# Mixture-of-experts stage: the small products between the weight slots, in four groups an expert

## The reference

```python
def swiglu(h, w_gu, w_down):
    gt, up = jnp.split(h @ w_gu, 2, axis=-1)
    return (jax.nn.silu(gt) * up) @ w_down

def moe(h, w_r, b_r, w_gu, w_down):
    t = h.reshape(-1, shp[-1])
    logits = (t @ w_r).astype(jnp.float32) + b_r.astype(jnp.float32)
    top_v, top_i = lax.top_k(logits, TOP_K)          # TOP_K = 2
    wts = jax.nn.softmax(top_v, axis=-1)
    comb = jnp.sum(jax.nn.one_hot(top_i, N_EXPERTS) * wts[..., None], axis=1)
    out = jnp.zeros_like(t)
    for e in range(N_EXPERTS):                       # 8 experts
        out = out + comb[:, e:e + 1] * swiglu(t, w_gu[e], w_down[e])
    return out.reshape(shp)
```

## Time and profile before

| what | value |
|---|---|
| median of three executions | 1933.45 us |
| the profiled execution, its time | 1935.77 us |
| its span, first to last instruction | 1933.7 us |
| mean granted clock of TensorE | 0.985 |
| TensorE matmul busy (whole program) | 1884.3 us, 97% |
| VectorE, ScalarE, GpSimd busy | 745.0, 453.5, 240.8 us |
| the eight experts | 946.15 to 1908.94 us of the span |

### The profile page before, as it was taken

The page is one execution under the profiler, slowest core; times in us unless marked ns, Lnnn a source line. Parts: engine busy times, 40 slices in busy tenths (PEclk is TensorE's granted clock), DMA queues, the critical chain, the costliest instruction groups (busy, mean ns, idle before and its releaser), DMA issues.

```text
span 1933.7 us, 55829 instructions
## 1 busy us (share of the span) xinstructions
PE 1884.3 (97%) x25022; PEld 1383.8 (72%) x25022; DVE 745.0 (39%) x1602; ACT 453.5 (23%) x852; POOL 240.8 (12%) x281
## 2 busy tenths in 40 slices
PE   7999999999999999999999999999999999999997
PEld 3777998999998778998655566555665556655564
DVE  5896448655584896357500101001010010100112
ACT  2214335445432215343300100101001000010011
POOL 2540423000003450432100000000000000000000
PEclk9999998999999999999999999999999999999998
DMA  9576445555552465445599999999999999999992
GB/s 357 181 268 246 142 159 175 196 185 176 183 180 93 144 218 198 146 137 186 205 376 392 361 375 337 376 392 361 375 336 378 393 357 375 335 379 398 361 365 70
DMA packets 143141, 525.48 MB, mean 272 GB/s; under 512 B 16192, under 2 KB 16704, under 8 KB 142272
## 3 DMA queue, kind: packets, MB, share of 16 engines
q1 hardware_dynamic: 140544, 508.82, 71.8%
q10 hardware_dynamic: 1728, 7.85, 1.2%
q0 software_dynamic: 640, 5.35, 0.8%
HBM read 515.52 MB, written 6.43 MB: 270 GB/s over the span
## 4 chain that ended last, share of the span: by engine, by line
PE 92%; DVE 4%; DMA 1%; issue 1%; ACT 1%; SPq 0%; ACTq 0%; DVEq 0%
PE bank L1057 46%; PE bank L913 13%; PE bank L297 9%; PE bank L653 8%; PE bank L517 4%; PE bank L533 2%; PE bank L999 2%; PE bank L1067 1%; PE bank L482 1%; PE bank L1010 1%; DMA masks<-in_masks 1%; PE bank L897 1%; PE bank L459 0%; PE bank L727 0%; DMA ring<-in_w 0%
## 5 line engine op out<-in xcount | busy, mean ns | idle before, releaser
L1057 PE MATMUL bank<-ring,gx 128*32 128x256 f32 x10752 | 599.9, 380 | 0.0
L1057 PEld LDWEIGHTS bank<-ring,gx 128*32 128x32 f32 x10752 | 340.0, 110 | 228.5 <-issue 8.0
L1057 PE MATMUL bank<-ring,arena 128*32 128x256 f32 x5376 | 296.5, 379 | 0.0
L1057 PEld LDWEIGHTS bank<-ring,arena 128*32 128x32 f32 x5376 | 172.3, 110 | 114.2 <-issue 1.3
L2418 DVE TENSOR_TENSOR arena<-arena,bank 128x128 f32<-128x128 f32 x168 | 38.3, 283 | 487.6 <-ACT arena L1548 487.6
L297 PE MATMUL bank<-hT,ring 128*128 128x264 f32 x864 | 204.8, 397 | 4.5 <-issue 2.5
L297 PEld LDWEIGHTS bank<-hT,ring 128*128 128x128 f32 x864 | 166.3, 195 | 40.3 <-issue 11.4
L913 PE MATMUL bank<-hh,whi 128*128 128x264 f32 x448 | 128.6, 287 | 1.3 <-DVE hl L2449 1.0
L2329 DVE COPY arena<-bank 32x256 f32<-32x256 f32 x27 | 11.5, 427 | 301.6 <-PE bank L1057 301.3
L913 PE MATMUL bank<-hh,wlo 128*128 128x264 f32 x448 | 127.5, 285 | 0.0
L913 PE MATMUL bank<-hl,whi 128*128 128x264 f32 x448 | 127.4, 284 | 0.0
(11 more groups left out here) (425 smaller groups left out, 2684.8 us busy)
## 6 DMA issues: line engine op xcount, KB each, us to landing
ring<-in_w SPq DMA_DIRECT2D x964, 512.0 KB, 5.7
out_gdns<-arena POOLq DMA_DIRECT2D x2, 2048.0 KB, 8.3
arena<-in_gdn ACTq DMA_DIRECT2D x2, 1536.0 KB, 7.1
xT<-in_x ACTq DMA_DIRECT2D x1, 1056.0 KB, 9.2
out_y<-hT SPq DMA_DIRECT2D x4, 264.0 KB, 2.1
arena<-in_gdn ACTq DMA_DIRECT2D x2, 512.0 KB, 3.9
masks<-in_masks ACTq DMA_DIRECT2D x1, 512.0 KB, 11.3
cpk<-in_cpk SPq DMA_DIRECT2D x1, 512.0 KB, 6.6
```

The costliest lines, as they stand in the source:

```text
L1057: ins = pe.matmul(o[32 * j:32 * j + 32, 0:DQ], x(t), w[:, DQ * c:DQ * c + DQ], start=first, stop=last)
```

## The change

The small products are put together in four groups an expert (five in odd experts but the last): behind slot 4 the return of m = 0 to 4; behind slot 20 turns 0 and 1 and the return of m = 5 to 7; behind slot 36 turns 2 and 3 and DCT; behind down slot 4 (slot 60) turns 4 to 6 and, where another pair follows, gathers 0 and 1; behind down slot 8 (slot 64) gathers 2 and 3. The products of a group go to different banks (BACK_BANK, TURN_BANK, DCT_BANK, GATHER_BANK), some of them banks of the chunk that is not being written, so new waits stand ahead of chunks 1, 3 and 5 and of the down slots. `erow` gets a third buffer. Expert 0 returns nothing, and the last expert gathers nothing; the zeroed rows and weights ahead of expert 0 are gone. (The further passes keep both.)

```diff
-        TURN = 3
         ROWS = 0
-        COMBINE = range(4, 8)
-        DCT = 9
+        BACK = {4: (0, 1, 2, 3, 4), 20: (5, 6, 7)}
+        BACK_BANK = (6, 7, 3, 4, 5, 3, 4, 5)
+        TURN = {20: (0, 1), 36: (2, 3), UP_S + 4: (4, 5, 6)}
+        TURN_BANK = (6, 7, 6, 7, 6, 7, 0)
+        DCT, DCT_BANK = 36, 3
-        GATHER = range(UP_S + 6, UP_S + 14, 2)
+        GATHER = {UP_S + 4: (0, 1), UP_S + 8: (2, 3)}
+        GATHER_BANK = (1, 2, 6, 7)
...
             for e in range(NE):
-                body(e, e, e // 2, e, e % 2, None)
-            body.finish(NE)
+                body(e, e - 1, e // 2, e, e % 2, None)
+            body.finish(NE - 1)
...
@@ TensorE: gather, combine
-                    if i >= 2:
-                        pe.wait_ge(sem("gx_done"), pg * 4 + (i - 1))
...
-                    pe.wait_ge(sem("down_taken"), g * KD + (KD + m - 1))
...
@@ TensorE: expert
+                returns = a is not None or q > 0
+                ahead = a is None and sub and e < NE - 1
...
+                def between(s):
+                    if TURN.get(s, (0,))[0]:
+                        pe.wait_ge(sem("turned_done"), q * NCH + TURN[s][0])
+                    for c in TURN.get(s, ()):
+                        turn(c)
+                    if s in BACK and BACK[s][0] == 0 and sub == 0:
+                        pe.wait_ge(sem("gx_done"), pg * 4 + 4)
+                    for m in BACK.get(s, ()) if returns else ():
+                        self.combine(m, g, bank[BACK_BANK[m]])
+                    if s == DCT:
+                        pe.wait_ge(sem("dw_done"), g * 3 + 6)
+                        for t in range(3):
+                            m = P if t < 2 else NB
+                            ins = pe.transpose(bank[DCT_BANK][0:CAP, P * t:P * t + m], dw[0:m, t, :], ident[0:m, 0:m])
+                        ins.then_inc(sem("dcT_full"), 1)
+                    if ahead and s in GATHER:
+                        if GATHER[s][0]:
+                            pe.wait_ge(sem("turned_done"), q * NCH + 6)
+                        for i in GATHER[s]:
+                            self.gather(i, pg + 1)
...
-                    if c == 1 and k == 0:
+                    if c == 1 and k == 0 and returns:
                         pe.wait_ge(sem("e_ys"), g * 2 + 2)
+                        pe.wait_ge(sem("down_taken"), g * KD + (KD + 5))
...
+                    if c == 3 and k == 0 and returns:
+                        pe.wait_ge(sem("down_taken"), g * KD + 2 * KD)
+                    if c == 5 and k == 0:
+                        pe.wait_ge(sem("dcT_done"), q * 1 + 1)
                     slot_products(s, lambda t: gx[:, k, mine + 32 * t:mine + 32 * t + 32], k == 0, k == KD - 1)
-                    if k == TURN and c:
-                        turn(c - 1)
...
+                    between(s)
                 for f in range(FT):
...
                     if f == 0:
-                        pe.wait_ge(sem("dcT_done"), q * 1 + 1)
+                        pe.wait_ge(sem("act_done"), q * NCH + (FT + 1 + NCH - 1))
...
+                    between(s)
@@ ScalarE, VectorE: the same lists, one slot later
-                    for c in turned_after(m):
+                    for c in TURN.get(m - 1, ()):
...
-                    if m - 1 in COMBINE:
-                        for k in (2 * (m - 1 - COMBINE[0]), 2 * (m - 1 - COMBINE[0]) + 1):
-                            self.add(k, g)
+                    for k in BACK.get(m - 1, ()) if a is not None or q else ():
+                        self.add(k, g, bank[BACK_BANK[k]])
...
-                        if sub:
+                        if a is None and sub and e < NE - 1:
                             self.choose(e + 1, a)
```

More of the change, by code:

```diff
@@ L224, in trunk_program @@
         at_e = 2 * B1 + NCH * TT * P
-        erow = ar(at_e, 2, TT, P)
-        srow = ar(at_e + 2 * TT * P, 2, TT, P)
-        ys = ar(at_e + 4 * TT * P, D)
+        erow = ar(at_e, 3, TT, P)
+        srow = ar(at_e + 3 * TT * P, 2, TT, P)
+        ys = ar(at_e + 5 * TT * P, D)
         ring2 = over("ring2", [P, ERING - RING, SLOT * P], where(whi), 0, F32)
-        yh = over("yh", [P, D], arena_at, at_e + 5 * CH)
+        yh = over("yh", [P, D], arena_at, at_e + 6 * CH)
         yl = over("yl", [P, D], slab_at, QT * (3 + N) + KD * N + 4)
[L231 to L234, removed]
+        dcT = over("dcT", [P, N], arena_at, at_e + 6 * CH + D)
+        dsel = over("dsel", [P, 3, PAIR], arena_at, at_e + 6 * CH + D + N)
+        dw = ar(at_e + 6 * CH + D + N + 3 * PAIR, 3, CAP)
+        iota = ar(at_e + 6 * CH + D + N + 3 * PAIR + 3 * CAP, PASSES * CAP)
         def col(l, name, i=0, w=None):
@@ L1002, in gather, with combine @@
                     ins.then_inc(sem("gather_full"), 1)
-                def combine(self, m, g):
+                def combine(self, m, g, b):
                     if m == 0:
                         pe.wait_ge(sem("ye_done"), g * 2 + 2)
-                    pe.wait_ge(sem("down_taken"), g * KD + (KD + m - 1))
-                    pe.matmul(bank[6 + m % 2][:, 0:N], yh[:, m * P:(m + 1) * P], dcT[:, :], start=True, stop=False)
-                    pe.matmul(bank[6 + m % 2][:, 0:N], yl[:, m * P:(m + 1) * P], dcT[:, :],
+                    pe.matmul(b[:, 0:N], yh[:, m * P:(m + 1) * P], dcT[:, :], start=True, stop=False)
+                    pe.matmul(b[:, 0:N], yl[:, m * P:(m + 1) * P], dcT[:, :],
                               start=False, stop=True).then_inc(sem("down_full"), 1)
                 def begin(self, g, pg, a):
-                    for i in range(4):
-                        self.gather(i, pg)
+                    if a is None:
+                        for i in range(4):
+                            self.gather(i, pg)
                 def end(self, g, a):
                     for m in range(KD):
-                        self.combine(m, g)
+                        pe.wait_ge(sem("down_taken"), g * KD + (KD + m - 1))
+                        self.combine(m, g, bank[6 + m % 2])
                     pe.wait_ge(sem("down_taken"), g * KD + 2 * KD)
@@ L1063, in turn @@
                     pe.wait_ge(sem("act_done"), q * NCH + (FT + 1 + c + 1))
-                    if c:
-                        pe.wait_ge(sem("turned_done"), q * NCH + c)
                     for r in range(TT):
-                        ins = pe.transpose(bank[6][:, P * r:P * r + P], erow[:, c % 2, r, :], ident)
+                        ins = pe.transpose(bank[TURN_BANK[c]][:, P * r:P * r + P], erow[:, c % 3, r, :], ident)
                     ins.then_inc(sem("turned_full"), 1)
+                def between(s):
[18 more added lines that the diff above has]
+                            self.gather(i, pg + 1)
+                if a is not None and sub == 0:
+                    for i in range(4):
+                        self.gather(i, pg)
                 mine = CAP * sub
@@ L1074, in expert @@
                     if sub == 0 and c == 0 and k % 2 == 0:
-                        pe.wait_ge(sem("gx_done"), pg * 4 + (k // 2 + 1))
-                    if c == 1 and k == 0:
+                        pe.wait_ge(sem("gx_done"), pg * 4 + max(k // 2 + 1, 2))
+                    if c == 1 and k == 0 and returns:
                         pe.wait_ge(sem("e_ys"), g * 2 + 2)
+                        pe.wait_ge(sem("down_taken"), g * KD + (KD + 5))
                     if c >= 2 and k == 0:
                         pe.wait_ge(sem("act_done"), q * NCH + (FT + 1 + c - 1))
+                    if c == 3 and k == 0 and returns:
+                        pe.wait_ge(sem("down_taken"), g * KD + 2 * KD)
+                    if c == 5 and k == 0:
+                        pe.wait_ge(sem("dcT_done"), q * 1 + 1)
                     slot_products(s, lambda t: gx[:, k, mine + 32 * t:mine + 32 * t + 32], k == 0, k == KD - 1)
-                    if k == TURN and c:
-                        turn(c - 1)
[L1083 to L1094, removed]
+                    between(s)
                 for f in range(FT):
@@ L1524, in begin @@
                 def begin(self, g, pg, a):
-                    for i in range(4):
-                        self.gathered(i, pg)
+                    if a is None:
+                        for i in range(4):
+                            self.gathered(i, pg)
                 def end(self, g, a):
@@ L1541, in expert @@
                 for m in range(FFN_S + 1):
-                    if m == ROWS:
+                    if m == 0 and a is not None and sub == 0:
+                        for i in range(4):
+                            self.gathered(i, pg)
+                    if m == ROWS and (a is not None or q):
                         self.rows(g, q, a)
@@ L2325, in rows @@
                     v.wait_ge(sem("ywt_done"), g + 1)
[L2326 to L2327 removed]
+                    v.wait_ge(sem("e_used"), q * FFN_S)
                     for r in range(TT):
@@ L2338, in low, with add @@
```

(17 more changed lines are left out.)

42 lines of the change are left out of this document (17 added, 25 removed).

## The result

The changed kernel takes 1901.95 us (median); before it are 1932.6 us (1931.24 to 1934.53). The ratio is 0.9838 with a 95% interval of 0.9824 to 0.9852, so the change is worth about 31 us. 1904.5 was forecast, within 1900 to 1914. The ratio leaves out one of the four executions of the changed kernel, which ran at a lower clock and took 2082.3 us; the median counts it.

The account below looks back on a forecast made before the run. TensorE, not the loads, was taken to bound the expert stage. Dropped products 9.9 us plus fewer breaks 20.9 less switches 1.8 gave 29.0 us saved, so 1904.5 us from a median of 1933.45, range 1900 to 1914.

Parts of the forecast that it names:

- The bound: Expert stage: TensorE binds, busy 962.67 of 962.79 us, not the loads; loads becoming the bound had chance 0.05.
- 366 and 377 GB/s: Load rates reckoned for all 672 slots (352.3 MB) over the expert stage, before and after the change.
- the prediction's estimate by that rule: At about 358 GB/s from HBM the expert stage could not be shorter than 984 us, so no gain.
- Products that fall away: Expert 0's returns (3.3 us) and the last expert's gathers (6.6 us) fall away: 9.9 us saved on TensorE.
- Breaks that fall away: Between slots in the experts: 104 breaks costing 31.1 us become 34 at 0.30, some 10.2 us; 20.9 us saved.
- switches inside a group: 18 places where transposes change to another product within a group: 0.1 us each, 1.8 us given back; bounds 0 to 5.4.
- New waits: Ahead of chunks 1, 3, 5 and the gather behind slot 60: all hidden, slack 2.7 us at chunk 1, about 3 at chunk 5.
- The experts: Length of each expert after the change: expert 0 near 112.5 us, even ones near 115, odd ones near 120.5.
- The sum: Whole expert stage: 9.9 + 20.9 - 1.8 = 29.0 us saved; the sum as it stands had chance 0.82.
- The slower rival: Ahead of slot 8, seven experts: 3 us stall plus 3.4 us from half clock each, 45 us, 1949 us; chance 0.03.

Follow-up runs that it names:

- two_thirds: Changed kernel with the last four of the twelve products of every slot left out, loads unchanged; stage 862.65 us, time 1834.57 us (one run).
- old_places: Changed kernel with every small product back at its former place and bank, dropped products still dropped; stage 952.77 us, time 1927.02 us, ratio 0.9954.
- late_return: Changed kernel with the first return group behind slot 7 instead of slot 4, directly ahead of chunk 1; stage 944.74 us, time 1916.46 us (one run).
- late_return_long: Changed kernel with the first return group behind slot 7 and eight useless VectorE copies behind the first add; stage 977.40 us, time 1953.15 us (one run).

## Why the prediction was right

- *The bound.* TensorE, not the loads: 931.40 of 931.40 us busy, and the ceiling of the loads lies at 408 GB/s (two_thirds), where the changed stage moves 373. The prediction's 366 and 377 GB/s are too high, since 14 of the 672 slots lie in the ring when the stage begins; the windows have 361 and 373. The rule of the Trainium skill on the HBM side (page DMA: Bandwidth & Descriptors, section Where 436 GB/s comes from), about 358 GB/s for a core, does not hold for a core that runs alone here: 373 GB/s over the changed stage, and 408. With the 345.0 MB that are loaded within the stage the prediction's estimate by that rule is 964 us and not 984, so that the length of the stage before, 963 us, did not by itself speak against it.
- *Products that fall away.* Forecast 9.9 us, measured 9.90 (old_places).
- *Breaks that fall away.* Forecast 20.9 us for 70 breaks at some 0.30, less 1.8 for 18 switches inside a group; measured 21.37 for both. The term that was mis-sized is the switch. Expert 0 shows turns 0 and 1 alone behind slot 20; this group costs there 0.92 us (942.13 to 970.27 less 21 slots of 1.296: 28.14 - 27.22). In expert 2 six combine products stand behind the turns, 0.72 us of work, and the group costs 1.65: the switch from transposes to combines costs about 0.01 us and not 0.1. The row that the 0.1 was taken from is no price of its own: here too the first step of the combines is long (0.21 us, 1204.15 to 1204.36), and the group as a whole is not.
- *New waits.* None shows. The slack ahead of chunk 1 is 2.95 us (2.7 forecast), ahead of chunk 5 3.0 (about 3).
- *The experts.* Expert 0 takes 112.32 us (942.13 to 1054.45; near 112.5 forecast), expert 1 120.21 (1054.45 to 1174.66; near 120.5), expert 2 114.57 (near 115).
- *The sum.* The stage fell by 31.3 us, 29.0 were forecast: 1.8 for the switches, 0.5 for breaks of 0.305 instead of 0.30. That is 0.5 past the 30.8 us to which the switches' bounds alone reached. The rest of what moved the profiled execution lies outside the stage, within the scatter of the nine profiles.
- *The slower rival.* Its mechanism exists, its size was off: a standstill of 1.8 us in each of seven experts had no second price (late_return); one of 4.5 us had 14.6 us in sum (late_return_long), 2.1 each in the mean and not the 3.4 that I had taken from the end of the kernel, since the half clock falls in part into the standstill itself and does not last equally long each time. The standstill of 3 us that the rival was reckoned with was not run.

What stays open: the 34 breaks that are left still cost some 10 us. Whether combines and gathers in 32-column strips would save a part of them was not tried on the chip.

## What to carry to other kernels

An engine that is 100% busy may still lose time: compare the length of stretches with and without a foreign step, and divide what is left into the step's own pace and a fixed price; here that price was 0.3 us for each change between products in strips and products of full width, and its sum over 70 breaks was told from three kinds of rows to 2% (20.9 us forecast, 21.37 measured). Group work of one kind where the buffers (here eight banks) allow it, and put a group so that the steps which wait for its results come three slots later, with an eye on what stands ahead of those steps in their own engine's queue. When the work around a stage drifts with the clock by some us, judge a change by the length of the stage.

## What the runs showed of the hardware

- A product of 32 columns put between products in the same strips costs 0.06 us; one of full width 0.46, of which some 0.24 (an estimate) are the change of width.
- TensorE's slot products take weights at 404 GB/s (512 KB in 1.296 us), 1% below the 408 GB/s at which the loads are at their ceiling. With a third less work a slot the stage is 863 us and waits for the loads; the 345.0 MB loaded within it alone take 846 us at 408 GB/s (an estimate), so savings on TensorE end about there.
- Seven standstills of 1.8 us left the granted clock at 1.00; each of seven standstills of 4.5 us took it down for a time (0.51 to 0.75 over 6.9 us), at 2.1 us each in the mean beside the standstill.
